# A four-sub-layer LayerNorm trunk: pieces behind each norm reordered on VectorE and ScalarE, sixteen unread products in two waits, recurrent states loaded later

## What is computed

```
for l in range(DEPTH):
    mod = (cs @ w_ada[l] + b_ada[l])[:, None, :]
    sh1, sc1, g1, sh2, sc2, g2 = jnp.split(mod, 6, axis=-1)
    h = x * (1.0 + sc1) + sh1
    ...
    x = layer_norm(ALPHA * x + (1.0 + g1) * y, ln_w[l, 0], ln_b[l, 0])
    h = x * (1.0 + sc2) + sh2
    y = jnp.square(jax.nn.relu(h @ w_up[l])) @ w_down[l]
    x = layer_norm(ALPHA * x + (1.0 + g2) * y, ln_w[l, 1], ln_b[l, 1])
```

## Time and profile before

| | us |
|---|---|
| median of 3 runs (3205.23 to 3209.25) | 3206.18 |
| the profiled execution | 3201.68 |
| its span, first to last instruction | 3199.9 |
| PE matmul busy | 3068.5 (96%) |
| VectorE busy | 1757.2 (55%) |
| ScalarE busy | 1305.6 (41%) |
| GpSimd busy | 297.6 (9%) |
| mean granted TensorE clock | 0.982 of full |
| mean DMA rate | 214 GB/s |

### The profile page before, as it was taken

The page is one execution under the profiler, slowest core; times in us unless marked ns, Lnnn a source line. Parts: engine busy times, 40 slices in busy tenths (PEclk is TensorE's granted clock), DMA queues, the critical chain, the costliest instruction groups (busy, mean ns, idle before and its releaser), DMA issues.

```text
span 3199.9 us, 66344 instructions
## 1 busy us (share of the span) xinstructions
PE 3068.5 (96%) x26924; PEld 2866.2 (90%) x26924; DVE 1757.2 (55%) x2470; ACT 1305.6 (41%) x1701; POOL 297.6 (9%) x290
## 2 busy tenths in 40 slices
PE   6899999989999999999999899999989999999998
PEld 3689998878899999999998788887979999999997
DVE  2477776664644444444446566666575444454546
ACT  1355555543433333333334444444354343343433
POOL 0022211111300000000001301100120000000000
PEclk8999999999999999999999899999989999999999
DMA  9998778887687676676776665665435555555552
GB/s 348 327 299 257 247 251 256 261 283 250 208 283 239 205 242 225 221 246 206 246 238 197 216 230 154 201 227 185 145 112 165 165 165 166 166 168 166 166 165 76
DMA packets 541640, 685.65 MB, mean 214 GB/s; under 512 B 22225, under 2 KB 469257, under 8 KB 541065
## 3 DMA queue, kind: packets, MB, share of 16 engines
q1 hardware_dynamic: 484402, 625.43, 60.0%
q10 hardware_dynamic: 56960, 56.21, 5.3%
HBM read 650.88 MB, written 30.67 MB: 213 GB/s over the span
## 4 chain that ended last, share of the span: by engine, by line
PE 85%; DVE 6%; DMA 5%; ACT 3%; issue 2%; SPq 0%; ACTq 0%; DVEq 0%; POOL 0%; POOLq 0%
PE main L543 25%; PE main L545 24%; PE main L544 24%; PE bank L555 4%; DMA raw<-in_w_ada 2%; DMA gl_s<-in_state_gla 1%; DVE w_lo L1809 1%; PE bank L679 1%; DVE z L2294 1%; DMA raw<-in_hg_w_out 1%; DVE z L2290 1%; ACT w_hi L1240 1%; ACT ln_h L1266 0%; DVE a_lo L2326 0%; DVE hg_s L2064 0%
## 5 line engine op out<-in xcount | busy, mean ns | idle before, releaser
L1809 DVE TENSOR_TENSOR w_lo<-raw,w_hi 128x1024 fp32r<-128x1024 f32 x804 | 994.1, 1237 | 1215.0 <-ACT w_hi L1240 1211.1
L1240 ACT ACTIVATE w_hi<-raw 128x1024 fp32r<-128x1024 f32 x804 | 850.5, 1060 | 1556.6 <-PE main L545 1460.4
L543 PE MATMUL main<-a_hi,w_hi 128*128 128x288 f32 x4272 | 1301.4, 305 | 43.4 <-DVE a_lo L2326 25.2
L545 PE MATMUL main<-a_hi,w_lo 128*128 128x288 f32 x4272 | 1269.2, 297 | 0.0
L544 PE MATMUL main<-a_lo,w_hi 128*128 128x288 f32 x4272 | 1268.3, 297 | 0.0
L543 PEld LDWEIGHTS main<-a_hi,w_hi 128*128 128x128 f32 x4272 | 812.2, 190 | 86.0 <-issue 36.1
L544 PEld LDWEIGHTS main<-a_lo,w_hi 128*128 128x128 f32 x4272 | 811.8, 190 | 4.4 <-issue 1.7
L545 PEld LDWEIGHTS main<-a_hi,w_lo 128*128 128x128 f32 x4272 | 811.5, 190 | 0.0
L543 PE MATMUL main<-act_hi,w_hi 128*128 128x288 f32 x2048 | 606.3, 296 | 0.0
L545 PE MATMUL main<-act_hi,w_lo 128*128 128x288 f32 x2048 | 604.9, 295 | 0.0
L544 PE MATMUL main<-act_lo,w_hi 128*128 128x288 f32 x2048 | 601.9, 294 | 0.0
(11 more groups left out here) (315 smaller groups left out, 2001.0 us busy)
## 6 DMA issues: line engine op xcount, KB each, us to landing
raw<-in_w_ada SPq DMA_DIRECT2D x384, 512.0 KB, 6.4
raw<-in_w_up SPq DMA_DIRECT2D x256, 512.0 KB, 3.8
raw<-in_w_down SPq DMA_DIRECT2D x256, 512.0 KB, 3.4
raw<-in_hg_w_in SPq DMA_DIRECT2D x128, 512.0 KB, 6.8
raw<-in_gla_w_in SPq DMA_DIRECT2D x100, 512.0 KB, 3.8
raw<-in_hg_w_out SPq DMA_DIRECT2D x32, 512.0 KB, 5.2
gl_s<-in_state_gla ACTq DMA_DIRECT2D x32, 512.0 KB, 6.3
out_new_gla_sample<-gl_s ACTq DMA_DIRECT2D x32, 512.0 KB, 4.7
```

The lines of the kernel that those rows point to most:

```text
L543: mm(out, hi, x_hi[:, kb, :], start=kb == 0, stop=False)
L545: last = mm(out, lo, x_hi[:, kb, :], start=False, stop=kb == KB - 1)
L1240: F(w_hi[:, st.split_slot(g)].rearrange("p k n -> p (k n)"), raw[:, slot, :], ACT.Copy).then_inc(hi_ready, 1)
L1809: V.tensor_tensor(w_lo[:, s].rearrange("p k n -> p (k n)"), raw[:, slot, :], w_hi[:, s].rearrange("p k n -> p (k n)").bitcast(F32), ALU.su ...
```

## The change

It has three parts.

- Behind norms 0, 1 and 2 the order of work is another. On VectorE each long `shift` moves ahead of the low part or the split of the piece before, `low(1)` moves ahead of the scaling of piece 2, and each split of a weight tile moves between a piece and its low part. On ScalarE the casts move with them: tile 3 ahead of piece 2, tile 4 ahead of piece 3, tiles 5 and 6 ahead of piece 4. Where the stage is LOW, tile 6 stays last.
- Behind the statistics of norms 2 and 3, which have no `filler`, PE multiplies ones by ones sixteen times into bank 6. Nothing reads the results.
- The four state loads move from ahead of the first GLA iteration into its steps 8 to 11.

```diff
@@ -945,6 +945,10 @@
             if filler:
                 filler(0, RING)
+            else:
+
+                for _ in range(16):
+                    mm(b6[:, 0:P], ones[:, :], ones[:, :], start=True, stop=True)
@@ -1616,14 +1620,18 @@
-            for n in range(3):
-                h_piece(i, e, n)
+            h_piece(i, e, 0)
+            h_piece(i, e, 1)
             cast(casts, 0, 3)
+            h_piece(i, e, 2)
+            cast(casts, 0, 4)
             h_piece(i, e, 3)
-            cast(casts, 0, 4)
+            cast(casts, 0, 5)
+            if casts is not LOW:
+                cast(casts, 0, 6)
             h_piece(i, e, 4)
-            cast(casts, 0, 5)
-            cast(casts, 0, 6)
+            if casts is LOW:
+                cast(casts, 0, 6)
@@ -1735,6 +1743,8 @@
+                if not prev and 8 <= s <= 11:
+                    gl_load(0, s - 8)
@@ -1767,8 +1777,6 @@
         act.wait_ge(G["gk2_set"], 1)
-        for b in range(4):
-            gl_load(0, b)
         gl_iteration(0, False)
@@ -2312,8 +2320,6 @@
                 first, last = PIECES[n]
-                if n >= 2:
-                    shift(first, last)
                 scale(first, last)
@@ -2329,17 +2335,23 @@
             piece(0)
             piece(1)
             low(0)
+            shift(4, 8)
+            low(1)
             piece(2)
-            low(1)
+            shift(8, 12)
+            split(splits, 0, 3)
             low(2)
-            split(splits, 0, 3)
             piece(3)
+            split(splits, 0, 4)
+            shift(12, 16)
             low(3)
-            split(splits, 0, 4)
             piece(4)
+            split(splits, 0, 5)
+            if splits is not LOW:
+                split(splits, 0, 6)
             low(4)
-            split(splits, 0, 5)
-            split(splits, 0, 6)
+            if splits is LOW:
+                split(splits, 0, 6)
```

## The result

The changed kernel takes **3185.01 us**, the median of 4 runs (3183.49 to 3187.08), against 3205.7 for the kernel before beside it (4 runs). The ratio is 0.9934, with a 95% interval of 0.9916 to 0.9951. It is faster by 20.7 us; 21.7 were predicted. A second set of five runs on another chip gave 3181.66 and 0.9923 (0.9909 to 0.9937).

A forecast was written before the change was run, and what follows sets the result against it. PE, busy 3068.5 of 3199.9 us, bounds the kernel; only its waits and lower clock can be won. 10.9 + 5 + 4.3 + 1.5 = 21.7, from 3206.18 to 3184.5 us (0.70), range 3179.0 to 3194.0.

The forecast's parts named there:

- No rival: Rivals: half the gain, 3193 (0.18); GpSimd and VectorE block each other, 3231 (0.04); no difference, 3206 (0.03); more, 3179 (0.05).
- Norm 2: 10.9: Behind norm 2 the new order brings pieces 6.35 us apart, not 9.11; gain 10.9, about 3 of it clock.
- two engines that take turns: Behind the norms VectorE and ScalarE wait for each other, so a piece takes 9.11 us where PE needs 6.4.
- Norm 0: 5: Behind norm 0 the same chain, partly covered by adaLN products, gains 5 us, bounds 3 to 5.5.
- The wait of cast 6: Behind norm 0 ScalarE's cast 6, now ahead of piece 4, can wait for its tile; cost nothing to 2 us.
- Norm 1: 4.3 for the last tile: Behind norm 1 LOW's last tile, bound by low part 4, starts 4.3 us earlier.
- The 2.9 for the clock: Behind norm 1, 2.9 us more if PE's lower clock level goes; nothing was taken for it in the sum.
- w_gk2: 1.5: PE's 1.49 us wait for matrix w_gk2 goes when the state loads move; gain 1.5, at the least 0.
- Products: 4.2 us, hidden: The products into bank 6 take 4.2 us, 0.131 each, inside waits; worth 1.0 behind norm 2, 0 behind norm 3.
- The rival's price of 1.4 an instruction: Each of a piece's five VectorE instructions waits 1.4 us for GpSimd's affine; 25 us slower, 3231, chance 0.04.
- the rival decides from 0.55 an instruction on: From 0.55 us of GpSimd blocking per VectorE instruction, a piece is back at 9.11 us; rival's chance 0.04.
- The signs: Right: low-part waits fall from 25.2 to about 10 us. Wrong: ScalarE's h newly waits for a raw tile behind norm 0.

The follow-up runs named there:

- experiments 4: The changed kernel with casts and splits of tiles 3 to 6 back in their old places; 3193.18 us, ratio 0.9958 to the kernel before.
- experiment 5: The changed kernel with each long shift but the first directly ahead of its scaling, low(1) behind piece 2's samples; 3192.52 us, ratio 0.9958 to the kernel before.
- Experiment 6: The changed kernel with, behind norm 1 alone, casts 4 and 5 behind pieces 3 and 4, splits following; 3179.83 us, ratio 0.9913 to the kernel before.
- experiment 8: The changed kernel with cast 4 and split 4 later behind norm 1, and GpSimd's affine waiting for each norm's last low part; 3179.77 us, ratio 0.9916.
- experiments 6 and 7: The second of these: the changed kernel with GpSimd's affine waiting for the norm's last low part; 3183.24 us, ratio 0.9924 to the kernel before.

## Why the prediction was right, point by point

- **The total.** Forecast 3184.5, measured 3185.01; by steps 21.7, by stages 21.4. No rival came true, but that the sum fits so well is in part luck: behind norm 1 a gain that did not come and one that I had left out nearly cancel, and the 11.6 of norm 2 is 10.2 against another trace of the same code.
- **Norm 2: 10.9, measured 11.6 (or 10.2).** The chain came as worked out. Counted from the first long shift (2338.53), low parts 2 and 4 end at +8.7 and +21.0, foreseen +8.9 and +21.5. The scaling takes 1.35 where I took 1.5, so the spacing is 6.1, not 6.35. What I had not said is which of the moves does it: from tile 0 on, experiments 4 and 5 give 8.2 to the casts and splits and about 2 to the shifts, with or without the others. My story of two engines that take turns was true of VectorE, yet PE's largest loss, 5.59, was a split queued behind a low part.
- **Norm 0: 5, measured 5.3** (6.6 in the second trace; the means of three traces with the old code there and six with the new differ by 6.0). The wait of cast 6 that I named came, 6.56 long, and hid where I said that it could.
- **Norm 1: 4.3 for the last tile, measured none, and 1 at most from tile 0 on.** This step failed. I took the chain of norm 2 for norm 1 and overlooked that cast 4 there is the first tile of another stage, whose load is still under way; I had looked at that risk for norm 0 alone. The 2.9 for the clock, which I left out, came instead (2.8 in this pair of traces, 1.5 against two others). Experiment 6 confirms the cause: with cast 4 back behind piece 3 the last tile is 20.9 from tile 0, 4.8 less than before, where I had forecast 4.3.
- **w_gk2: 1.5, and 1.5 in this pair of traces.** As a price of part 3 it was mis-sized: alone it brings 5.4, and on top of the order 7.7, both by the ratios. I read one wait in one execution, and priced it as if PE would arrive as late as before. With the order changed PE is earlier, w_gk2 lands 12.9 after its issue in place of 6.0, the wait becomes 7.83, and the clock falls behind it.
- **Products: 4.2 us, hidden; measured 3.73, hidden.** 0.117 each, not 0.131. Worth behind norm 2 1.0, measured 0.3 from tile 0 on (1.4 in the opening as it stands, of which 1.1 arose ahead of the products); behind norm 3 nothing, and the tails with and without them are 25.2 to 25.4 and 25.3.
- **GpSimd and VectorE.** The rival's price of 1.4 an instruction is excluded, and I had its source wrong: 1.4 was the time of a GpSimd instruction that VectorE already held up. By itself it takes 0.58. VectorE loses nothing on a scaling or a shift in the change, at most 0.1 on a long low part and 0.2 to 0.3 on samples and splits, 0.36 being the most seen behind the norms in any trace here. That the rival decides from 0.55 an instruction on was not wrong, but it needs all five instructions of a piece to be held that long, and none was.
- **The signs.** Waits for low parts came to 16.3, not about 10: 11.7 of it behind norm 1, by the step that failed. And behind norm 0 ScalarE's h did stand for a raw tile, which I had called a sign of being wrong; it cost PE nothing that can be seen.

Of parts that add up: order alone by its ratio 14.1, states 5.4, products nothing, together 19.5 for a whole of 21.2 by its own ratio. The intervals hold both, but the traces show why they need not add: the order's gain behind norm 1 reaches the end only if w_gk2 is early.

Open: whether the total of experiment 8 is better than the change's, and why the statistics run at the lower clock in some traces and not in others. Keeping cast 6 behind piece 4 in norm 0 was not tried by itself.

## What to carry to other kernels

An in-order engine gives its next consumer what stands first in its queue, not what is needed first: list for each waiting tile which of its two inputs comes last, and put that one ahead, above all a short job that stands behind one which itself waits. When a consumer becomes earlier, look at the next thing it reads: a small load issued behind large ones on one queue turns the gain into a wait, and swapping two issues repairs it. And before a cast or load is moved ahead of critical work, look whether its own input has landed in every place where the shared code runs. When variants are compared by single traces, count from the first instruction behind what varies by chance: the openings of the change and of experiment 6 seemed to differ by 1.3, and both are 26.0 from tile 0 on.

## What the runs showed of the hardware

- A 16 KB transfer issued behind four of 512 KB on ScalarE's queue landed after 6.0, 8.4 and 12.9 us in three kernels; issued just ahead of the same four, or with them some 26 us later, after 5.2 to 5.8. Around it the DMA engines were full with the load of raw tiles as well: 363 GB/s where it took 12.9, 358 where it took 5.4.
- GpSimd's 128x288 instruction took 0.58 us by itself and up to 3.9 beside VectorE, whose 128x1024 and 128x1152 instructions ran on without a gap (two of GpSimd's in 4.51 us). VectorE's scalings and shifts stayed at 1.35 in the change, with single rows up to 1.66 in experiment 5; its 128x128 instructions went from 0.29 to between 0.32 and 0.56.
- Behind a wait of 5.32 ahead of which the statistics had run at the upper level, tile 0 ran at the lower one (0.61, then 0.44 a matmul, in place of 0.40 and 0.29). With 3.73 us of unread products in that wait it ran at the upper. In experiments 6 and 7, where the statistics were at the lower level, the products took 4.16 and 4.04, and tile 0 was at the upper again. Waits of about 2.8 were followed by 0.40 in some traces and by 0.61 in others.
- Behind a wait of 7.83 for a DMA the granted clock was 0.59 over the next 5 us, and the work up to the second gate product took 1.6 longer; behind one of 1.49 it was 1.00.
